# Recurrent branch's mixing begun right behind the causal weights, value pages and memory heads in a new order

## What is computed

```python
q_sb, k_sb, v_sb, q_mem, p_rw, g_sb, g_mem, g_rw = _split(x @ w_in, IN_SPLITS)
o_sb = sb_mix(...)       # causal stick-breaking attention; samples over 16 cached pages each
o_mem = _mem_attend(...) # softmax attention over 256 memory rows, 4 heads of 128
o_rw, shift, wkv = _rwkv7(p_rw, ...)
merged = (sigmoid(g_sb) * (o_sb @ w_sb_o) + sigmoid(g_mem) * (o_mem @ w_mem_o)
          + sigmoid(g_rw) * (o_rw @ w_rw_o))
h = _layer_norm(DN_ALPHA * x + merged @ w_out)
y = _layer_norm(DN_ALPHA * h + _moe(h, ...))   # 32 experts, top 4

def _rwkv7(...):
    prev = concatenate([shift0, p_rw[:, :-1]])
    xs = p_rw + mu_rw * (prev - p_rw)              # "mix"
    r, k, v, w_lo, a_lo, g_lo = _split(xs, RW_SPLITS)
    w_raw = w_decay0 + tanh(w_lo) @ w_decay2       # "dec"
    a = sigmoid(w_aaa0 + a_lo @ w_aaa2)            # "aaa"
    g = sigmoid(g_lo) @ w_gate2                    # "gr"
    kk = k * rw_k_k; kk = kk / sqrt(sum(kk * kk))  # head sums "kn"
    k_mod = k * (1 + (a - 1) * rw_k_a)
    ...
    bonus = sum(r * k_mod * rw_r_k) * v            # head sums "bon"
```

## Time and profile before

| | us |
| --- | --- |
| runs shown | 1525.96, 1522.55, 1524.51 |
| median | 1524.51 |
| profiled execution | 1529.42 |
| its span, first to last instruction | 1527.5 |
| mean granted clock of PE, share of full | 0.989 |

### The profile page before, as it was taken

How to read it: one execution, slowest core, us unless ns; L and a number is a source line. 1 busy time by engine, 2 the same in 40 slices (tenths; PEclk the granted TensorE clock), 3 DMA queues, 4 the chain that set the end, 5 groups by cost and what they waited for, 6 DMA issues and landing times.

```text
span 1527.5 us, 22221 instructions
## 1 busy us (share of the span) xinstructions
PE 1465.0 (96%) x8374; PEld 747.0 (49%) x8374; DVE 572.5 (37%) x994; ACT 265.7 (17%) x534; POOL 141.9 (9%) x267
## 2 busy tenths in 40 slices
PE   7998999899999999999999999999999999999995
PEld 6887645457777755434434434434434434434431
DVE  1999957824445643211211211211211211211214
ACT  1111523222212111111111111111111111111102
POOL 5332232230210101000000000000000000000000
PEclk9999999999899999999999999999999999999998
DMA  9899997994111457999999999999999999999994
GB/s 346 311 367 335 349 363 281 350 308 149 29 57 57 148 246 265 423 428 428 428 429 428 429 429 429 429 427 429 429 428 429 428 429 429 428 428 428 428 426 184
DMA packets 67898, 534.30 MB, mean 350 GB/s; under 512 B 8588, under 2 KB 9687, under 8 KB 35063
## 3 DMA queue, kind: packets, MB, share of 16 engines
q1 hardware_dynamic: 48774, 471.52, 74.7%
q0 software_dynamic: 8656, 41.97, 7.8%
q10 hardware_dynamic: 10400, 19.92, 3.6%
HBM read 528.92 MB, written 4.46 MB: 349 GB/s over the span
## 4 chain that ended last, share of the span: by engine, by line
PE 76%; DVE 8%; issue 7%; DMA 6%; ACT 2%; POOL 0%; POOLq 0%; DVEq 0%; SPq 0%; ACTq 0%
PE bank L814 73%; DVE ring L2002 5%; PE bank L815 3%; DMA early<-in_w_gate_up 2%; DMA arena<-in_w_gate_up 2%; DMA arena<-in_state_rw_wkv 1%; DVE early L2008 1%; DVE arena L2366 0%; ACT memT L1938 0%; DMA arena<-in_x_sample 0%; DVE arena L2342 0%; DVE arena L2460 0%; ACT arena L1666 0%; DVE arena L2070 0%; DVE arena L2351 0%
## 5 line engine op out<-in xcount | busy, mean ns | idle before, releaser
L814 PE MATMUL bank<-arena 64*64 64x64 f32 (+9 forms) x2738 | 290.7, 312 | 7.3 <-DVE arena L2077 2.2
L2568 DVE TENSOR_SCALAR arena<-bank 128x256 f32<-128x256 f32 x64 | 26.9, 421 | 629.9 <-PE bank L814 629.9
L814 PE MATMUL bank<-projT,ring 128*128 128x264 f32 x1056 | 255.0, 396 | 4.7 <-DMA ring<-in_w_in 1.9
L814 PEld LDWEIGHTS bank<-arena 64*64 64x64 f32 (+5 forms) x2738 | 183.5, 155 | 127.0 <-issue 114.8
L814 PE MATMUL bank<-ring,projT 128*64 128x512 f32 x1024 | 229.7, 595 | 0.9 <-DMA ring<-in_w_gate_up 0.9
L814 PEld LDWEIGHTS bank<-projT,ring 128*128 128x128 f32 x1056 | 198.8, 193 | 45.9 <-issue 4.1
L814 PE MATMUL bank<-ring,memT 128*64 128x512 f32 (+2 forms) x640 | 168.8, 603 | 5.8 <-ACT memT L1938 4.5
L814 PEld LDWEIGHTS bank<-ring,projT 128*64 128x64 f32 x1024 | 70.6, 137 | 149.9 <-issue 148.1
L814 PE MATMUL bank<-projT 128*64 128x512 f32 (+2 forms) x544 | 118.8, 581 | 0.4 <-DMA projT<-in_w_gate_up 0.4
L1934 ACT ACTIVATE arena<-arena 128x256 f32<-128x256 f32 x64 | 26.7, 417 | 410.8 <-DVE arena L2568 410.8
L814 PEld LDWEIGHTS bank<-ring,memT 128*64 128x64 f32 (+2 forms) x640 | 51.6, 143 | 81.5 <-issue 70.1
(11 more groups left out here) (291 smaller groups left out, 1073.5 us busy)
## 6 DMA issues: line engine op xcount, KB each, us to landing
ring<-in_w_gate_up SPq DMA_DIRECT2D x64, 2048.0 KB, 20.2
projT<-in_w_gate_up SPq DMA_DIRECT2D x32, 2048.0 KB, 21.1
ring<-in_w_down SPq DMA_DIRECT2D x32, 2048.0 KB, 24.6
arena<-in_w_gate_up SPq DMA_DIRECT2D x16, 2048.0 KB, 20.5
projT<-in_w_down SPq DMA_DIRECT2D x16, 2048.0 KB, 23.2
early<-in_w_gate_up SPq DMA_DIRECT2D x16, 2048.0 KB, 22.1
ring<-in_cache_sb_k SPq DMA_DIRECT2D x64, 256.0 KB, 6.1
ring<-in_cache_sb_k POOLq DMA_DIRECT2D x64, 256.0 KB, 5.7
```

The costliest lines, as they stand in the source:

```text
L814: mm = lambda out, l, r, first, last, **k: pe.matmul(out, l, r, start=first, stop=last, **k)
L2568: ts(g_, chunk[:, 0:512:2], LIMIT, None, ALU.min).then_inc(sem("g_ready"), 1)
```

## The change

Nothing of the arithmetic changes. What moves:

- DVE: `mix` writes its differences into `memT` (the memory rows' place, free once the memory values are projected) and not into `T1`, so it need no longer wait for the causal attention's buffers. `mix(12)`, which feeds the low-rank products, now stands behind `causal_weights(1)`; `mix(4)`, `mix(0)` and the squares follow ahead of the memory work. The cached scores of samples 2 to 7 stand later.
- PE: `dec`, `aaa` and `kn` come right behind value units 16 to 19, the value units run ahead of the memory heads, queries 4 to 7 stand behind the last value unit, `mzT` behind output step 72. Both `keep_warm` calls of the stretch are gone (2 and 6 products).
- SP: the load of `mK 1` stands behind unit 29 and not 25.
- ACT follows PE's order; its exponentials of `cum` stand behind the first four output tiles.

```diff
-    after_gate = {5: ("dec", "aaa", "gr"), 6: ("kn",), 7: ("bon",)}
+    after_gate = {4: ("dec", 0, "aaa", "kn"), 5: ("gr", 1), 7: ("bon", 2, 3)}
...
-                elif u == 25:
+                elif u == 29:
                     sp.wait_ge(*last_reader(("mK", 0)))
                     load_cache(("mK", 1))
...
-            g.wait_ge(sem("kk_sq"), 1)
+            g.wait_ge(sem("mixed"), 2)
...
-                    if t == 0 and nm == "dec":
-                        keep_warm(b, 2)
...
+            sample_values(10, 11)
             values(0)
-            sample_values(10, 11)
             values(1)
...
+            branches(36, 40)
             sample_values(14, 15)
-            branches(36, 40)
             sample_sum(2)
+            sample_values(16, 17)
+            memory_turn(0)
+            low_rank("dec")
             memory_query(1)
-            memory_turn(0)
+            sample_values(18, 19)
+            memory_values(0)
+            low_rank("aaa")
+            pe.wait_ge(sem("masks"), 7)
+            over_heads("kn", T1, "kk_sq")
+            sample_sum(3)
             branches(40, 44)
...
+            sample_values(28, 29)
+            branches(60, 64)
+            sample_sum(5)
+            over_heads("bon", T1, "rk_prod")
+            sample_values(30, 31)
             memory_turn(2)
+            sample_sum(6)
             memory_query(4)
-            branches(56, 60)
-            sample_values(24, 25)
             memory_values(2)
+            sample_sum(7)
+            memory_scores(3)
             memory_query(5)
-            branches(60, 64)
-            memory_scores(3)
-            sample_values(26, 27)
-            sample_sum(5)
-            over_heads("bon", T1, "rk_prod", early=6)
-            memory_turn(3)
-            memory_query(6)
-            sample_values(28, 29)
-            memory_values(3)
-            memory_query(7)
-            sample_values(30, 31)
-            sample_sum(6)
-            sample_sum(7)
...
+            memory_turn(3)
             row_to_features("so_sT", "so_s")
+            memory_query(6)
+            memory_values(3)
...
-            branches(64, 72)
+            branches(64, 68)
+            memory_query(7)
+            branches(68, 72)
+            pe.wait_ge(sem("zm"), 1)
+            b = start("mzT")
...
             causal_weights(1)
+            gone(v, "shift_in")
+            gone(v, ("mv", 0))
+            gone(v, ("mv", 1))
+            mix(12)
+            v.sem_inc(sem("mixed"), 1)
             keep_own(2)
...
-                d = T1[:, 0:n, :]
+                d = memT[:, 0:n, :]
...
+            mix(4)
+            mix(0)
             memory_max(0)
...
             link(per_tile(KK, Kx, KKp))
             tt_(T1, KK, KK, ALU.mult).then_inc(sem("kk_sq"), 1)
+            memory_norm(0)
+            cached_scores(0)
+            keep_own(3)
+            mix(8)
+            v.sem_inc(sem("mixed"), 1)
+            cached_scores(1)
+            keep_own(4)
...
+            memory_max(1)
             v.reciprocal(T2[:, 2, :], T2[:, 2, :])
-            cached_scores(5)
             link(v.reciprocal(T2[:, 3, :], T2[:, 3, :]))
             link(tt_(KK, KK, T2, ALU.mult))
+            memory_norm(1)
+            cached_scores(2)
...
             per_tile(T1, T1, RKp).then_inc(sem("rk_prod"), 1)
-            memory_max(3)
-            memory_norm(3)
+            keep_own(5)
+            cached_scores(3)
+            memory_max(2)
             keep_own(6)
+            memory_norm(2)
...
             link(tt_(AA, KK, AA, ALU.mult))
+            keep_own(7)
+            cached_scores(4)
+            memory_max(3)
...
             tt_(T2[:, :, 0:256], ...).then_inc(sem("cum"), 1)
+            cached_scores(5)
+            memory_norm(3)
             cached_scores(6)
             cached_scores(7)
-            keep_own(7)
```

117 lines of the change are left out of this document (46 added, 71 removed).

## The result

| | kernel before | changed kernel |
| --- | --- | --- |
| median, first comparison | 1525.24 us (4 runs) | 1543.62 us (4 runs, 1538.31 to 1547.32) |
| median, second comparison | 1529.99 us (31 runs) | 1543.94 us (10 runs) |
| ratio, first and second | | 1.0095 [1.0063, 1.0128], 1.0095 [1.0066, 1.0123] |
| profiled execution, its span | 1529.42, 1527.5 us | 1547.32, 1545.5 us |

The change makes the kernel about 1% slower, 14 us by the ratio (interval 10 to 19). I had forecast 3.3 us, and 1527.8 in a range of 1520 to 1532.5. The direction was right, the size was not, and the time lies far outside the range.

A forecast was written before the change was run, and what follows sets the result against it. PE was taken to bound the kernel (76% of the chain). Unit 31's end at 294.0 plus a 29.7 us tail plus 0.6 for hand-overs gave 324.3 against 320.96: 3.3 us later, 1527.8, range 1520 to 1532.5.

The forecast's parts named there:

- Early part: no gain: Units 10 and 11 ahead of `values(0)` turn PE's 2.18 us wait into a longer wait for unit 13's pages: 0.
- DVE's way to the load: `kn` starts near 247.5, `cached_scores(3)` ends near 276, SP's last issue behind the `mK 1` load is done near 284.4.
- Rival C: Queues collide in full: `kn` 2 us late, last pages land at 296; +7.5 us, 1532; chance 0.12.
- Landing: Last pages of units 30 and 31, sharing with POOL's outputs, land at 291.5; unit 31 ends near 294.0.
- PE's way to unit 30: PE comes to unit 30 at 284.8 instead of 306.1: 15.3 us gone, 7.9 moved behind, 1.9 added.
- The tail: From unit 31's end to step 80: 29.7 us in place of 11.5, PE idling some 7 on DVE's norm.
- The clock: Two drops to half clock behind PE's long waits, about 1.7 and 1.3 us; without any, 3.0 lower, 1524.8.
- A: Faster: pages land in time, unit 31 ends at 287.5 to 289.5; 4.4 us earlier, 1520.1; chance 0.22.
- B: Even: pages near 289.5 and one clock drop less; 1524.5 to 1525.5; chance 0.20 with D.
- D: `mix` in `memT` would still wait for something late; chance 0.02, time as in B.

The follow-up runs named there:

- a_same: The changed kernel once more, nothing altered, for a second profile: 1543.94 us, ratio 1.0095 to the kernel before.
- b_mix: The kernel before with only `mix` writing into `memT` and `mix(12)` behind `causal_weights(1)`: 1528.72 us, ratio 0.9999 to the kernel before.
- a_warm12: The changed kernel with three dummy products ahead of value unit 12 alone: 1540.00 us, ratio 1.0081 to the kernel before.
- a_out_late: The changed kernel with POOL's six outputs of keys and values held back until value unit 30 is computed: 1534.03 us, ratio 1.0040 to the kernel before.
- a_turn: The changed kernel with memory heads 2 and 3 ahead of units 30 and 31 on PE, DVE and ACT: 1528.11 us, ratio 1.0004 to the kernel before.
- a_turn_warm: The changed kernel with memory heads 2 and 3 ahead of units 30 and 31, and dummies ahead of units 12, 19 and 30: 1522.41 us, ratio 0.9958.
- a_warm: The changed kernel with dummy products ahead of units 12, 19 and 30 and of `memory_turn(3)`: 1539.05 us, ratio 1.0048 to the kernel before.
- a_k31: The changed kernel with SP's load of `mK 1` behind unit 31 and not 29: 1537.74 us, ratio 1.0047 to the kernel before.

## Why the prediction missed

**The sum by its own steps.** Times from the mark (215.58 before, 214.80 in `a_same`, 222.47 in the changed kernel's first trace):

| step | forecast | a_same | changed, first trace |
| --- | --- | --- | --- |
| `kn` starts | 31.9 | 36.9 | 37.9 |
| from there to DVE's clamp | 4.5 | 3.9 | 5.0 |
| clamp to the end of `cached_scores(3)` | 24.0 | 24.2 | 24.7 |
| issues of load and pages | 8.4 | 6.9 | 6.9 |
| last issue to the end of unit 31 | 9.6 | 13.0 | 12.3 |
| tail to `mpv` | 30.3 | 30.6 | 31.2 |
| sum | 108.7 | 115.6 | 118.2 |

The kernel before has 105.4. So the forecast was 3.3 us more, and the traces show 10.2 and 12.8.

*Early part: no gain.* The wait moved as the step said: 2.18 us became 3.22 us ahead of unit 12 in `a_same`. But the step came to 0, and it was a loss. The clock falls to half in that wait, and `memory_scores(0)`, behind the same work in both orders, starts 17.4 us behind the mark in `a_same` and 16.1 in the first trace, where the kernel before had 14.5. These 1.6 to 2.9 us come back in the next step. `b_mix` shows that `mix(12)` in its new place costs nothing.

*DVE's way to the load.* This step failed first. It moved `kn` up by the PE work that goes from ahead of it to behind it, and took no account of pages. But unit 19 stands ahead of `kn` with one memory value and `aaa` between, 4.7 us with the unit itself. A start at 31.9 asked for unit 19 at 27.2, and its pages let it begin at 31.5 to 32.3; in the kernel before, the last of them had landed at 27.5. The pages of units 18 and 19 are fetched only when units 14 and 15 have been used, and these end later in the new order: unit 15 at 23.2 us behind the mark in `a_same` and 21.7 in the first trace, 18.3 before. Ahead of them stand the loss of the early part and four gate steps (1.9 us) that used to stand behind. The row of units 14 and 15 in the kernel before, for the one at 236.06 in `a_same`:

```profile
231.99 1.92 PE L814 MATMUL bank<-ring,early 128*32 128x512 f32 x16
```

The kernel before had already shown PE waiting for pages here, at unit 13; the step on the early part used that row, and this step should have used it again. Worth 5 to 6 us. Rival C had `kn` late, by 2 us and by a clock drop at unit 12; `a_warm12` and the other traces with dummies there leave about 1 us for that. The chain behind `kn`, 24 us, was right to 0.7.

*Landing.* Mis-sized. From the last issue to the end of unit 31 it took 12.3 to 13.0 us where I had 9.6, for the pages took 10.5 us from issue to landing in the median. `a_out_late` shows that POOL's outputs do it, as the sum assumed in kind. The issues were 1.5 us shorter than forecast, since the load took 1.92 us to issue where the earlier trace rows had 3.75. I had cited the Trainium skill ("DMA: Bandwidth & Descriptors", section on queues, rings and completion order) for the engines' turns between queues. That agrees with `a_out_late`: with the outputs gone from the other queue, the same pages behind the same load land 3.3 us sooner in the median. It doesn't tell taking turns from another way of sharing.

*PE's way to unit 30.* Forecast at 69.2 behind the mark; in `a_same` PE is there at 76.4 (291.2), in the first trace at 80.3. 5 to 6 us of it are the late unit 19 again, the rest further short waits for pages and half clock. It hardly counts, as PE waits for the pages of unit 30 in both.

*The tail.* Right: 30.3 forecast, 30.6 and 31.2 measured, with the second wait at 7.00 us where I had some 7. And it is what makes the change slower: `a_turn` changes the order at this end alone, and the whole 14 us are gone. So the prediction had the decisive mechanism, and set against it a gain on PE's way to unit 31 that was too large: 15.5 us forecast (93.9 to 78.4), 8.9 measured in `a_same` and 6.9 in the first trace.

*The clock.* I had put in 3.0 us for two drops, against two before. In `a_same` there are three, of 23.9 us in all, in the first trace five, of 34.1, where two of 6.8 had been. The dummies of `a_turn_warm` give back 7 us by the ratio, those of `a_warm` likely as much. That step was low by half or more. In the table this loss lies inside the other rows. The Trainium skill ("TensorE: Matmul & The Clock Gate", on why this matters for your kernels) warns of idle gaps between bursts; the rows agree, with half clock behind waits of 3.22, 4.72 and 7.00 us.

**What stays open.** No version had `kn` ahead of unit 19: that the pages of unit 19 hold it is read from the traces, and not shown by moving it. The stretch in `a_same` is 10.2 us longer, the ratio says 14. The interval of the ratio, 10 to 19 us, just holds the 10.2, and that trace is of the shortest of ten executions; if the others lose more, no trace shows where. `a_warm` is 7 us faster by its runs and not in its trace. Why outputs beside the pages cost 8 us by the ratio, when unit 31 ends 5.4 us sooner without them, is open for the same reason.

**The rivals.** A put the end of unit 31 at 72 to 74 behind the mark; the earliest of any version was 78.0 (`a_k31`), so neither A nor B, which needed the pages nearly as early, came about. D falls with `kn`, which did come some 17 us sooner than before. C was nearest. It had the pages take the 8.9 us and more of the outputs, and they did (10.5 in the median). It also had `kn` late, but that came about mainly for another reason than C's.

The range was too narrow at its upper end for the same reason. It took bounds for the landing and for one clock drop, but allowed `kn`, the term on which all later ones stand, only the 2 us of rival C, and it was 5 to 6 us late.

## What to carry to other kernels

When a piece of work is moved ahead in an in-order queue, list what stands ahead of it in the new place and ask for each item when its data land: the piece can't come sooner than the latest of these, however much work was moved behind it. When an engine waits twice for late data near the end of a stretch, look for work that needs neither and stands between or behind the waits, and move it ahead of the first; here that was worth 14 us, and the load's place, once this was mended, nothing. Gains from two cures of one late load don't add up, so try them together before you count them.

## What the runs showed of the hardware

- The part of the span ahead of the mark is the same program in both kernels, and yet took 214.8 to 226.2 us in the executions profiled. Much of the difference is in PE's waits for weights between 98 and 154 us: the longest two were 4.21 and 5.91 us in the changed kernel's first trace and 1.20 and 2.86 in `a_same`. One profiled execution can't be compared with another as a whole; compare stretch by stretch.
- Four issues of 512 KB took SP 3.75 to 4.49 us in the three traces of the old order and 1.92 to 2.35 in the fourteen of the new, with the same line and sizes. Why is open.
- 2.1 MB of outputs from POOL's queue, started within 5 us of SP's last pages, took these from 7.0 to 8.6 us from issue to landing up to 10.2 to 12.0. POOL's own last two pages, issued ahead of the outputs, took some 6 us either way.
- Half clock ahead of a wait for data can be free: in `a_warm12`, without it, PE reached unit 19 no sooner than in `a_same` (32.15 and 32.28 us behind the mark).
